# A two-block fp32 network on one core: layer norms by column parts, filter steps inside weight units, routing gates moved behind the gate-branch additions, a memory norm applied at evacuation

## The reference

```python
def first_block(x, p, ln0_g, ln0_b, w_in, ...):
    h = layer_norm(x, ln0_g, ln0_b)
    for i in range(DEPTH):                      # DEPTH = 2
        u = h @ w_in[i]                         # 1024 -> 2560
        y_hy = hyena_mixer(u[..., :o_q], ...)   # filters: sin(sin(z @ fw1) @ fw2) @ fw3, normalised by energy
        y_att = diff_attention(...)
        y_pool = pool_mixer(...)
        mix = jnp.concatenate([y_hy, y_att, y_pool], axis=-1) @ w_out[i]
        h = layer_norm(DN_ALPHA * h + mix, ln1_g[i], ln1_b[i])
        y_moe = hier_moe(h, ...)                # 4 groups of 4 experts, 2 experts of one group per token
        y_ple = jax.nn.sigmoid(h @ ple_wg[i] + ple_bg[i]) * (p[i] @ ple_wp[i])
        h = layer_norm(DN_ALPHA * h + y_moe + y_ple, ln2_g[i], ln2_b[i])
    return h
```

## Time and profile before

| | us |
|---|---|
| median of 3 runs | 1678.33 |
| lowest, highest | 1674.76, 1679.82 |
| the profiled execution, device time | 1681.11 |
| its span | 1679.1 |
| PE busy (share) | 1532.0 (91%) |
| DVE busy | 1319.7 (79%) |
| ACT busy | 1024.2 (61%) |

### The profile page before, as it was taken

One profiled execution on the slowest core, in us unless ns is written; L12 is line 12 of the kernel. 1 busy time (PEld: TensorE's weight loads), 2 busy tenths in 40 slices (PEclk: granted clock), 3 DMA queues, 4 the chain that ended last, 5 costly groups with the idle time before them and its releaser, 6 DMA issues.

```text
span 1679.1 us, 21283 instructions
## 1 busy us (share of the span) xinstructions
PE 1532.0 (91%) x7230; PEld 1258.6 (75%) x7230; DVE 1319.7 (79%) x1943; ACT 1024.2 (61%) x1491; POOL 95.4 (6%) x187
## 2 busy tenths in 40 slices
PE   5997999979888999989969999999789969999998
PEld 4876887858767778768867888887677658888786
DVE  6756799887668998876678999988775468999887
ACT  4543577645535776637446777766575437777775
POOL 4002000030022000000200000000000100000000
PEclk9998999989999999999979999999899879999999
DMA  9433599965435899754546999989441329999985
GB/s 325 133 107 115 184 337 343 309 216 187 131 103 187 278 341 310 275 188 138 164 129 233 366 359 363 364 291 335 149 148 59 103 71 312 359 360 361 360 294 208
DMA packets 282874, 402.82 MB, mean 240 GB/s; under 512 B 16026, under 2 KB 220538, under 8 KB 282512
## 3 DMA queue, kind: packets, MB, share of 16 engines
q1 hardware_dynamic: 273632, 381.99, 67.2%
q0 software_dynamic: 9136, 19.48, 3.8%
HBM read 400.37 MB, written 1.05 MB: 239 GB/s over the span
## 4 chain that ended last, share of the span: by engine, by line
PE 77%; DVE 15%; ACT 5%; issue 3%; DMA 1%; DVEq 0%; POOL 0%; ACTq 0%; SPq 0%; POOLq 0%
PE bank L623 21%; PE bank L625 21%; PE bank L624 21%; DVE w_lo_at L1939 4%; PE bank L640 2%; ACT w_hi_at L1401 2%; PE bank L759 1%; PE bank L786 1%; PE bank L920 1%; DVE x_at L1994 1%; PE bank L1321 1%; PE bank L669 1%; PE bank L1320 1%; DVE t_lo_at L1946 1%; PE bank L670 1%
## 5 line engine op out<-in xcount | busy, mean ns | idle before, releaser
L1939 DVE TENSOR_TENSOR w_lo_at<-raw_at,w_hi_at 128x1024 fp32r<-128x1024 f32 (+1 forms) x730 | 852.6, 1212 | 95.7 <-ACT w_hi_at L1401 86.4
L1401 ACT ACTIVATE w_hi_at<-raw_at 128x1024 fp32r<-128x1024 f32 (+1 forms) x730 | 726.1, 1046 | 159.3 <-PE bank L625 128.2
L623 PE MATMUL bank<-w_hi_at,xs_hi_at 128*128 128x512 f32 x800 | 326.5, 408 | 18.3 <-DVE xs_lo_at L2172 6.3
L625 PE MATMUL bank<-w_hi_at,xs_lo_at 128*128 128x512 f32 x800 | 318.2, 398 | 0.0
L624 PE MATMUL bank<-w_lo_at,xs_hi_at 128*128 128x512 f32 x800 | 316.8, 396 | 0.0
L623 PE MATMUL bank<-w_hi_at,t_hi_at 128*128 128x512 f32 (+3 forms) x528 | 208.8, 395 | 10.2 <-DVE t_lo_at L1946 5.2
L624 PE MATMUL bank<-w_lo_at,t_hi_at 128*128 128x512 f32 (+3 forms) x528 | 202.7, 384 | 0.0
L625 PE MATMUL bank<-w_hi_at,t_lo_at 128*128 128x512 f32 (+3 forms) x528 | 202.7, 384 | 0.0
L623 PEld LDWEIGHTS bank<-w_hi_at,xs_hi_at 128*128 128x128 f32 x800 | 152.9, 191 | 51.0 <-issue 13.8
L625 PEld LDWEIGHTS bank<-w_hi_at,xs_lo_at 128*128 128x128 f32 x800 | 152.9, 191 | 34.6
L624 PEld LDWEIGHTS bank<-w_lo_at,xs_hi_at 128*128 128x128 f32 x800 | 153.0, 191 | 30.7
(11 more groups left out here) (500 smaller groups left out, 1735.0 us busy)
## 6 DMA issues: line engine op xcount, KB each, us to landing
raw_at<-in_moe_w_dram SPq DMA_DIRECT2D x192, 512.0 KB, 5.3
raw_at<-in_moe_w_gate_dram SPq DMA_DIRECT2D x128, 512.0 KB, 5.2
raw_at<-in_moe_w_up_dram SPq DMA_DIRECT2D x128, 512.0 KB, 6.6
raw_at<-in_moe_w_down_dram SPq DMA_DIRECT2D x128, 512.0 KB, 5.5
raw_at<-in_w_in_dram SPq DMA_DIRECT2D x40, 512.0 KB, 6.7
raw_at<-in_a_w_in_dram SPq DMA_DIRECT2D x20, 512.0 KB, 4.6
raw_at<-in_w_out_dram SPq DMA_DIRECT2D x16, 512.0 KB, 4.2
raw_at<-in_ple_wg_dram SPq DMA_DIRECT2D x16, 512.0 KB, 5.3
```

The source lines that it names most:

```text
L623: pe.matmul(out, ah, bh, start=start, stop=False, skip_group_check=loose)
L625: return pe.matmul(out, al, bh, start=False, stop=stop, skip_group_check=loose)
L1401: act.activation(WH[:, s.part(), a], RAW[:, s.slot(), a], ACT.Copy).then_inc(hi_half[i], 1)
L1939: dve.tensor_tensor(WL[:, s.part(), a], RAW[:, s.slot(), a], WH[:, s.part(), a].bitcast(F32), ALU.subtract).then_inc(split_half[i], 1)
```

## The change

It changes the order and the grain of work in layers 0 and 1, and a little in layer 2's start:

1. ln0's gain and bias go by SP to one partition each and are broadcast by four PE matmuls into banks 0 to 3; DVE reads them from there. POOL's load of the window (`WIN`) and all later ones of layer 0 wait for the first half of ln0.
2. ln0, ln1 of both layers and ln2 of layer 0 go through `norm_and_turn`: columns 0 to 511 first, which PE transposes at once; then columns 512 to 1023, whose transposes stand in the middle of the first unit.
3. The second filter product is in the middle of unit 1, the third in the middle of unit 2, the energy in the middle of unit 3.
4. The addition of the second mixed strip waits for unit 13 and not for unit 14; ACT converts one more unit ahead of ln1; the evacuation of `ple_wp` comes after the first transposes.
5. The logits come after unit 15, their transposition in the middle of unit 16, `ranks` after it. On DVE `add_rows(0)` comes before the two best, `add_rows(1)` after them, gate weights and table after the gathered tokens; the exponential becomes two sigmoids. PE's `key_row` and `gates` move behind the first unit of expert 1.
6. MEM is multiplied by its gain alone; its squares are summed on ACT in expert 2 of pass 0; the inverse root multiplies keys and values when they leave PSUM.

```diff
@@ gpsimd, sync
+            for slot, n in enumerate(("ln0_g", "ln0_b")):
+                sp.dma_start(ROW[0:1, slot, :], A[n].rearrange("(a n) -> a n", a=1)).then_inc(*first_rows.tick("ln0"))
-            rows("ln0", [(A["ln0_g"], 0, 0), (A["ln0_b"], 1, 0)], None)
...
                 param("filt", L, FW3[:, :], A["hy_fw3"][L])
+                if L == 0:
+                    pool.wait_ge(*dve_ready.at(("h_a", 0)))
                 param("filt", L, WIN[:, :, :], A["c_win"])
@@ tensor: experts
+                if L < DEPTH:
+                    pe.wait_ge(*turn_lo.at((("h1", L), 1)))
+                    claim(0, 1)
+                    unit_by_token((0, 1), lambda c: c, True, False,
+                                  mid=lambda: turn(("h1", L), X, DC, [dve_ready.at(("ln1", L))], groups=(2, 3), banks=H1_BANKS))
+                    pe.wait_ge(*turn_lo.at((("h1", L), 3)))
                 pe.wait_ge(*dve_ready.at(("rw", L)))
...
-                    claim(0, 1)
-                    unit_by_token((0, 1), lambda c: c, True, False, mid=turn_logits)
+                    unit_by_token((0, 1), lambda c: 4 + c, False, True, mid=turn_logits)
+                    owner[0] = owner[1] = evac_d.at((f"ple_g{L}", 0))
                     ranks()
-                    unit_by_token((0, 1), lambda c: 4 + c, False, True)
...
+                        if (p, e) == (0, 1):
+                            key_row()
+                            gates()
@@ tensor: start and layer
+            pe.wait_ge(*first_rows.at("ln0"))
+            for half in range(2):
+                for slot in range(2):
+                    ins = pe.matmul(BK[2 * half + slot][:, :], ONES[0:1, :], ROW[0:1, slot, 512 * half:512 * half + 512],
+                                    start=True, stop=True)
+            ins.then_inc(*small_ready.tick("ln0_rows"))
...
-                turn(("h", L), X, DC, [dve_ready.at("ln0" if L == 0 else ("ln2", 0))])
+                turn(("h", L), X, DC, [dve_ready.at(("h_a", L))], groups=(0, 1), banks=(4, 5, 4, 5))
...
+                pe.wait_ge(*turn_lo.at((("h", L), 1)))
+                claim(0, 1)
+                unit_by_token((0, 1), lambda c: c, True, False,
+                              mid=lambda: turn(("h", L), X, DC, [dve_ready.at(("h_b", L))], groups=(2, 3), banks=(4, 5, 4, 5)))
...
+                unit_by_token((0, 1), lambda c: 4 + c, False, True, mid=second_filter)
...
+                unit_by_token((2, 3), lambda c: c, True, False, mid=third_filter)
...
+                unit_by_token((2, 3), lambda c: 4 + c, False, True, mid=energy)
...
-                turn(("h1", L), X, DC, [dve_ready.at(("ln1", L))])
-                pe.wait_ge(*turn_lo.at((("h1", L), 3)))
+                turn(("h1", L), X, DC, [dve_ready.at(("ln1_a", L))], groups=(0, 1), banks=H1_BANKS)
                 experts(L)
@@ scalar
+                            if (p, e) == (0, 2) and L == DEPTH - 1:
+                                act.wait_ge(*params_in["mem"].at(0))
+                                for half in range(2):
+                                    for tb in range(TB):
+                                        n = 2 * half + tb
+                                        ch.do(act.activation(SROW[:, 0:512], MEM[:, tb, 512 * half:512 * half + 512], ACT.Square,
+                                                             accum_out=SS[:, n:n + 1]))
+                                act.nop().then_inc(*act_ready.tick("ssmem"))
...
-                act.wait_ge(unit_used, s.count(-1))
+                split()
+                root(("ln1", L), 2)
+                act.wait_ge(*params_in["route"].at(L))
+                act.activation(RWHL[:, :, 0:NR[L]], RW[:, :, 0:NR[L]], ACT.Copy).then_inc(*act_ready.tick(("rwh", L)))
+                turn(("h1", L), DC, TH, banks=H1_BANKS, groups=(0, 1))
+                act.wait_ge(unit_used, s.count(-2))
@@ vector
+            def norm_and_turn(key, rows, first, last, turned_key, banks=(4, 5, 4, 5), row=row_of):
+                do(dve.tensor_scalar(RS[:, 0:TB], MV[:, 0:TB, 1], LN_EPS, None, ALU.add))
+                variance(key)
+                dve.wait_ge(*rows)
+                shift(X, 0, row)          # 2 x 128x512
+                rooted(key, TB)
+                scale(X, 0, row)          # 2 x 128x512
+                done(first)
+                shift(X, 1, row)
+                turn(turned_key, DC, TH, TL, banks=banks, groups=(0, 1))
+                split()
+                sync()
+                scale(X, 1, row)
+                done(last)
...
-                table()
                 if L < DEPTH:
-                    split()
                     dve.wait_ge(*rows_in.at(("ple", L)))
                     add_rows(0)
-                    split()
+                    two_best()
                     split()
                     add_rows(1)
+                    split()
                     done(("ple_b", L))
...
                 if L < DEPTH:
                     split()
-                if L == DEPTH - 1:
-                    dve.wait_ge(*params_in["mem"].at(0))
-                    measure(MEM)
-                    mean_squares()
-                    variance("memn")
+                    weights()
+                    table()
...
-                    dve.wait_ge(unit_used, s.count(strip - 2))
+                    dve.wait_ge(unit_used, s.count(-2))
...
+            do(dve.tensor_tensor(RS[:, TB:2 * TB], SS[:, 0:TB], SS[:, TB:2 * TB], ALU.add))
+            do(dve.tensor_scalar(RS[:, TB:2 * TB], RS[:, TB:2 * TB], 1.0 / D, EPS, ALU.mult, ALU.add))
...
+            do(dve.tensor_copy(RSM[:, :], RS[:, TB:2 * TB]))
+            done("mem_root")
```

267 lines of the change are left out of this document (126 added, 141 removed).

## The result

The changed kernel takes 1658.81 us (median of six, 1656.81 to 1665.56), the kernel before 1676.55 (six). The recorded ratio is 0.9907, with a 95% interval of 0.9887 to 0.9927: 0.9% faster, on the 1678.33 of the forecast about 1662.7. The forecast was 1655.2 with a range of 1646 to 1668. The direction and the two large terms were right. The gain was some 14 to 16 us by the two ratios, 17.7 and 12.8 us by the medians, where 23 was forecast.

A forecast was written before the change was run, and what follows sets the result against it. PE, 91% busy, was taken as the bound, so only its idle time or earlier starts count. Terms -10.0 - 10.6 - 1.1 - 2.1 + 0.65 = -23.15 us took the median 1678.33 to 1655.2, range 1646 to 1668.

The forecast's parts named there:

- the two large terms: Layer 0 from ln1 to the experts, -10.0 us, and layer 1 with ln1 and the memory statistics, -10.6 us.
- ln1 (-9.9 and -9.0 with routing -0.9): Earlier addition and halves at ln1: unit 18 ends 9.9 us earlier in layer 0; layer 1's first expert matmul 9.0 earlier.
- Routing order: Reordered DVE work between unit 18 and the experts: first expert matmul 6.05 us after unit 18 instead of 7.0.
- The start (-1.1): Layer 0's start: rows broadcast by PE and ln0 in halves, 1.1 us less, ends +1.5 and -3.5.
- Start of layer 1 (-2.1): Norm before layer 1 by halves: first unit at 366 instead of 369.1, 2.1 us less, ends -0.5 and -3.5.
- Gates (+0.85): DVE's gate weights and table moved behind the gathered tokens: 0.85 us per layer reaches PE in the experts.
- MEM (-3.6, +1.1, +0.65): Layer 1 experts: DVE statistics removed, -3.6 us; squares on ACT and gain, +1.1; second block's root operations, +0.65.
- (a): Chain from logits to experts keeps its 27.2 us; each layer gains 5.5 us less: -12, 1666 us; chance 0.08.
- (b): Gain taken back in the experts by the weight transfers and DVE: 1675 us, no change; chance 0.04.
- (c): Gate weights in the experts cost 3.6 us per layer instead of 0.85: +5.5, 1660.8 us; no chance of its own.
- (d): Short PE waits around split ln1 keep the clock low through units 15 to 18: 21 us per layer, 1697; chance 0.03.

The follow-up runs named there:

- first trace: The changed kernel without edits, its first profiled execution: span 1654.4 us; median 1658.81 us, ratio 0.9907 to the kernel before.
- second trace: The changed kernel run again without edits, on another chip: span 1659.9 us, median 1661.74 us, ratio 0.9918 to the kernel before.
- whole rows: The changed kernel with ln1 shifted and scaled over both halves before the first transposes: ratio 0.9975 to the kernel before.
- the one with 6.48: The changed kernel with the second mixed strip's addition waiting for unit 14 again: ratio 0.9969 to the kernel before.

## Why the prediction was right in sign and too large

- **ln1 (-9.9 and -9.0 with routing -0.9): right.** PE's wait came out as 1.04 (forecast 1.0). The stretch to the first expert matmul fell by 11.5 in layer 0 (10.8) and by 9.5 or, with a low stretch, 7.6 in layer 1 (9.0). Each of the two steps was undone singly and cost what the mechanism says. That unit 15 began 3.74 after unit 14 (3.8) was in part luck: the eight transposes took 1.09 where 1.85 was put in, and the wait for their low part 1.61 where it was 0.95. And part of the gain is the clock, which the forecast took in without naming it: it put the logits at 2 us, where they had taken 3.4 at the low level, and they took 1.87.
- **Routing order: right**, 5.9 us from unit 18 to the experts (6.05), 1.1 less than before. With gates and table in front it is 7.4, so their place carries it; the place of the two additions was not tried by itself.
- **The start (-1.1): wrong, +1.8 and +3.7.** Three parts failed. The broadcast was taken as 3.4 to 6.9 us between the two clock levels and lay just past the slow end (7.19), so the first transposes came at 17.48 where 15.1 was forecast. "Its reader is the filter after unit 2, so it should be hidden": f1 waits for all loads of its group, and the window is in it. The window itself took 3.2 us to landing, near the 3.1 of the earlier trace rows and above the estimate of 2.6. And "filter products and the energy in the middle of units" was credited with about 0.3 per stall without naming what stands behind them on DVE: 0.87 and 0.94 us of waiting ahead of the second transposes of attention, one in each layer. Of the +1.8 of the first trace unit 0's start is -0.05, the eight transposes that now stand in it make units 0 to 3 0.9 longer, and 1.0 is that wait. The +3.7 of the second trace has 1.9 of low stretches more.
- **Start of layer 1 (-2.1): too large.** The whole stretch to unit 14 is 0.6 shorter; the halves gave 2.1 (7.62 instead of 9.76 of waiting), but from the transposes to the end of unit 3 it took 0.3 more, as unit 0 now waits 0.94 for its low weights, and attention took 1.2 more, 0.94 of it the wait that the energy makes.
- **Gates (+0.85): mis-sized in layer 0**, +2.8: 0.37 is DVE's gate weights and table, 0.79 is PE's two products, which the forecast put at "nothing" because they are as long as before (their place costs, not their length), and 1.6 is a stretch of matmuls 0.43 apart behind the wait that is not in every trace. In layer 1 the 0.79 is there as well and the 0.37 is not.
- **MEM (-3.6, +1.1, +0.65): right.** The first expert stretch of layer 1 fell by 2.6 including the gates (2.75 forecast), or by 1.0 in the second trace, which has a low stretch there. The squares show as 10.60 instead of 9.52 between the third and fourth transposes, the third memory unit waited 5.62 instead of 5.31. That the stretch to it did not grow comes from a low stretch of 1.8 us among the experts of the kernel before that the later traces lack.
- **Rivals.** (a) and (b) did not come: the chain from the logits to the experts shortened from 27.2 to 20.7 us (189.78 - 169.10), and the experts held PE's 97%. (c) came near by its number in layer 0 (+2.8 of 3.6), but DVE's gate weights are only 0.37 of that. (d) came in part. At ln1 of layer 0 the three short waits left the clock at 2.4 GHz in all eleven traces that have them (1.00 from 156 to 172), and the one longer wait of whole rows lost it. At ln1 of layer 1 the same waits (1.04 and 1.68 around the first transposes) were followed by 11 matmuls at the low distance in six of the eleven, 2 us each time; the 21 us per layer of (d) never came. The rule of the Trainium skill (TensorE: Matmul & The Clock Gate, A second HAM failure mode: psum-queue depth-cycling) that frequent small idle times make the clock swing is thus not borne out at ln1 of layer 0; in layer 1 and behind the 0.8 to 1.2 us wait in the experts some traces agree with it. The forecast's price for (d) was also misread: a low stretch 12 us longer costs some 6 us, as 24 matmuls lose 4.8 us in 10.3, so it would have taken about 25 us per layer to lose the whole gain.

## What to carry to other kernels

Of a step moved into the middle of another, follow the engine that reads its result: what it does next, and who waits for that, is the price. The same holds for a small product put right ahead of the instruction that needs it: two products "as long as before" cost 0.79 us of waiting by their new place. A load that shares a semaphore with others holds back the first reader of any of them. Where a stage is split so that one long wait becomes several short ones, count the clock too: here the waits of 3.7 us and 6.5 us at ln1 were followed by a low stretch each time. The split ln1 and the wait of about 1 us in the experts were followed by one in 22 of 47 cases, 6 of 22 at ln1 and 16 of 25 in the experts.

## What the runs showed of the hardware

- A wait of 3.70 us was followed by a longer low stretch than one of 6.48, in both layers of the one trace of each: 11 matmuls at the low distance against 6. In layer 0 they are at the high distance again from 165.2 in the one with 6.48, still at the low one at 166.0 in the one with 3.70.
- The clock stayed low while PE was busy without a gap (0.50 from 1307 to 1316 in the kernel before, with PE busy for all of the 9.00 us); the last wait, 1.07 us, had ended at 1303.07.
- In the first units of a run the matmuls are 0.43 apart although the granted clock of the window is given as 1.00 (22 to 25 us in the changed kernel: eight matmuls in 3.00 us); there the distance of starts is what to read.
- Four fp32 products of one row by 512 columns took 7.19 us at the start of the run, 0.9 for each of their eight instructions, in each of the twelve traces that have them.
